# A short first block, a reordered preparation of the scan, GpSimd held back behind two projections, and mLSTM gating one chunk later

## The reference, cut to what matters

```python
z, xbc, dt = jnp.split(h @ w_in, [SSM_D_INNER, SSM_D_INNER + SSM_CONV_DIM], axis=-1)
dt = jax.nn.softplus(dt.astype(f32) + dt_bias.astype(f32))
a = dt * A                        # per head; a_cs = cumsum over a chunk of 128 tokens
decay_to_end = jnp.exp(a_cs[..., -1:] - a_cs)
...
x = x + rmsnorm(y, post_norm[i])  # behind the projections out of mamba and of attention
...
h = num / jnp.maximum(jnp.abs(den), jnp.exp(-m_t))[..., None]        # mLSTM
mh = rmsnorm_2(mh, mlstm_norm_w) * jax.nn.sigmoid(m_o)
```

## Time and profile before

| | |
|---|---|
| median of 3 runs | 2681.82 us (2678.59 to 2682.61) |
| profiled execution, its own time | 2678.74 us |
| span in the profile | 2677.0 us |
| PE, DVE, POOL, ACT busy | 2320.1, 1568.4, 1502.8, 714.9 us |

### The profile page before, as it was taken

One profiled execution on the slowest core, in us unless ns is written; L12 is line 12 of the kernel. 1 busy time (PEld: TensorE's weight loads), 2 busy tenths in 40 slices (PEclk: granted clock), 3 DMA queues, 4 the chain that ended last, 5 costly groups with the idle time before them and its releaser, 6 DMA issues.

```text
span 2677.0 us, 28363 instructions
## 1 busy us (share of the span) xinstructions
PE 2320.1 (87%) x9216; PEld 1519.9 (57%) x9216; DVE 1568.4 (59%) x3381; ACT 714.9 (27%) x1935; POOL 1502.8 (56%) x1060
## 2 busy tenths in 40 slices
PE   8999899899989999789988888888777777777776
PEld 7888678788978879677754443444232223222222
DVE  1266592333431668632387878887778776555555
ACT  2111553214422131423222222222223222111112
POOL 7777377676567754264665656555544444344331
PEclk9999899999989999899999999999999999999999
DMA  4222002222222210031289999999999999999996
GB/s 146 93 95 94 17 1 93 91 100 80 103 88 87 86 63 1 1 110 48 100 339 408 421 421 421 421 413 421 421 422 422 421 421 422 421 422 421 421 421 258
DMA packets 105898, 646.35 MB, mean 241 GB/s; under 512 B 12720, under 2 KB 15152, under 8 KB 39600
## 3 DMA queue, kind: packets, MB, share of 16 engines
q0 software_dynamic: 73728, 536.90, 48.3%
q1 hardware_dynamic: 31776, 106.87, 11.6%
q10 hardware_dynamic: 272, 1.05, 0.1%
HBM read 640.58 MB, written 4.19 MB: 241 GB/s over the span
## 4 chain that ended last, share of the span: by engine, by line
DMA 32%; PE 10%; DVE 5%; POOL 2%; issue 1%; ACT 1%; POOLq 0%; DVEq 0%; ACTq 0%
DMA peer_row<-in_peer_uv,peer_ids 32%; PE bank L3156 7%; DVE peer_row L3101 3%; PE bank L281 2%; POOL peer_row L3078 1%; PE bank L2850 1%; POOL w_parts L229 1%; ACT peer_diag L3135 1%; DVE peer_weight L3093 1%; PE bank L2811 0%; POOL w_parts L227 0%; DVE peer_top_i L2669 0%; DVE peer_picked L2742 0%; DVE peer_sc_left L2672 0%; DVE peer_top_v L2665 0%
## 5 line engine op out<-in xcount | busy, mean ns | idle before, releaser
L3156 PE MATMUL bank<-peer_row,peer_diag 128*128 128x512 f32 x2048 | 966.8, 618 | 266.7 <-ACT peer_diag L3135 264.5
L3078 POOL DMA_INDIRECT peer_row<-in_peer_uv,peer_ids x512 | 585.8, 1144 | 645.6 <-PE bank L3156 604.4
L3156 PEld LDWEIGHTS bank<-peer_row,peer_diag 128*128 128x128 f32 x2048 | 380.0, 194 | 823.5 <-ACT peer_diag L3135 430.0
L3101 DVE CUSTOM_DVE_ANT_0 peer_row<-peer_row,peer_h_tok 128x1024 f32<-128x1024 f32 x512 | 641.0, 1256 | 329.2 <-DMA peer_row<-in_peer_uv,peer_ids 328.3
L208 POOL TENSOR_TENSOR w_parts<-ring,zero 128x1024 fp32r<-128x1024 f32 x156 | 295.5, 1894 | 227.5 <-PE bank L281 112.4
L211 POOL TENSOR_TENSOR w_parts<-ring,w_parts 128x1024 fp32r<-128x1024 f32 x156 | 374.4, 2400 | 29.0 <-POOL w_parts L208 29.0
L3139 ACT ACTIVATE peer_acts<-peer_dots 128x2 f32<-128x2 f32 x256 | 52.1, 204 | 734.0 <-DVE peer_dots L3101 734.0
L3135 ACT ACTIVATE peer_diag<-ident,peer_weight 128x128 f32<-128x128 f32 x512 | 177.5, 394 | 223.8 <-DVE peer_weight L3093 221.1
L257 PE MATMUL bank<-ssm_h_high,w_parts 128*128 128x512 f32 x512 | 157.7, 389 | 0.8 <-DVEq L644 0.8
L257 PEld LDWEIGHTS bank<-ssm_h_high,w_parts 128*128 128x128 f32 x512 | 96.1, 188 | 20.9 <-DVEq L644 1.0
L257 PE MATMUL bank<-hyb_h_high,w_parts 128*128 128x512 f32 x320 | 99.9, 393 | 0.8 <-DVEq L644 0.8
(11 more groups left out here) (559 smaller groups left out, 3803.8 us busy)
## 6 DMA issues: line engine op xcount, KB each, us to landing
ring<-in_weights SPq DMA_DIRECT2D x180, 512.0 KB, 3.2
peer_row<-in_peer_uv,peer_ids POOLq DMA_INDIRECT x512, 25.4
resid<-in_x SPq DMA_DIRECT2D x4, 512.0 KB, 7.6
out<-resid SPq DMA_DIRECT2D x4, 512.0 KB
xa_mem<-in_mem ACTq DMA_DIRECT2D x1, 1024.0 KB, 4.9
xa_kept<-xa_v_out SPq DMA_DIRECT2D x1, 1024.0 KB
xa_kept<-xa_k_out SPq DMA_DIRECT2D x1, 1024.0 KB
xa_v<-xa_kept SPq DMA_DIRECT2D x1, 1024.0 KB, 5.3
```

The lines of the kernel that those rows point to most:

```text
L3078: pool.indirect_dma_start(self.rows[row][:, :], None, self.m.ins["peer_uv"], bass.IndirectOffsetOnAxis(ap=self.choice.ids[:, t, slot:slot ...
L3101: dot = dve.tensor_tensor_reduce(mine, mine, self.tokens(slot_of(j)[0]), 1.0, 0.0, ALU.mult, ALU.add, self.dots[:, h % 4, r:r + 1])
L3156: mm = pe.matmul(self.m.banks[2 * t + half][:, :], self.diag[:, j % (2 * GROUP), :], self.rows[row][:, D + half * 512:D + (half + 1) * 512 ...
```

## The change

It has four parts, and none of them changes what is computed.

1. `set_up` keeps two loads, the first quarter of the tokens and `cols`; nothing waits for `cols` there, ACT does in the next block. All other loads are issued in `mamba_in`, the second quarter now ahead of the first unit. The three small rows for the scan are loaded there too.
2. The preparation of the scan uses seven banks for the transposes; DVE takes the tiles 0 to 3 and the even ones, ACT the odd ones from 5. The bias is added first of all, PE's sums stand behind tile 13, and the exponentials stand between the copies.
3. Behind the two projections GpSimd splits four units by `split_ahead`. Between the high and the low part of the first it waits for the four additions. In the second place the split of the small weight comes after these four units.
4. In mLSTM GpSimd begins to gate chunk t when chunk t + 1 has its denominator.

```diff
-def split_ahead(m, pool, n, parts=None):
+def split_ahead(m, pool, n, parts=None, pause=None):
...
         pool.wait_ge(m.w_high, u + 1)
+        if pause is not None and u == m.split:
+            pool.wait_ge(*pause)
         pool.tensor_tensor(low, m.ring[:, u % RING, :], high, ALU.subtract).then_inc(m.w_split, 1)
...
@@ set_up
-            for n in range(4):
-                here = slice(n * D // 4, (n + 1) * D // 4)
-                sp.dma_start(m.resid[:, :, here], x[:, :, here]).then_inc(m.x_loaded[n], 16)
-                if n == 0:
-                    sp.dma_start(m.cols[:, :], m.ins["cols"]).then_inc(loaded, 16)
-                    sp.dma_start(m.ring[:, 0, :], m.ins["weights"][0]).then_inc(m.w_loaded[0], 16)
-            stream_weights(m, sp, RING)
-            sp.wait_ge(loaded, 16)
+            load_tokens(m, sp, 0)
+            sp.dma_start(m.cols[:, :], m.ins["cols"]).then_inc(m.cols_loaded, 16)
...
@@ mamba_in
+            load_tokens(m, sp, 1)
+            sp.dma_start(m.ring[:, 0, :], ins["weights"][0]).then_inc(m.w_loaded[0], 16)
+            for n in (2, 3):
+                load_tokens(m, sp, n)
+            stream_weights(m, sp, RING)
             sp.dma_start(raw.w[:, :, :], ins["ssm_w_dt"]).then_inc(raw.loaded, 16)
+            for n, name in enumerate(("ssm_dt_bias", "ssm_a_log", "ssm_d")):
+                sp.dma_start(rows[:, n, :], m.row(name, HEADS)).then_inc(rows_loaded, 16)
             stream_weights(m, sp, 4 * ZC + CM_T)
+            sp.wait_ge(rows_loaded, 48)
...
@@ mamba_scan, PE
-                    if j >= 4:
-
-                        pe.wait_ge(by_act if j % 2 else by_dve, (j - 4) // 2 + 1)
+                    before = j - len(turn_banks)
+                    if before >= 0:
+                        pe.wait_ge(by_dve if dve_takes(before) else by_act, taken(before))
...
+                    if j == SUMS_AFTER:
+                        pe.wait_ge(dve_dt, 3)
...
@@ mamba_out_attention_in, gpsimd
             split_weights(m, pool, kt)
-            split_weights(m, pool, project.units)
+            split_ahead(m, pool, RING, pause=(out.added, TT))
+            split_weights(m, pool, project.units - RING)
...
@@ attention_out_hybrid_in, gpsimd
             split_weights(m, pool, kt)
+            split_ahead(m, pool, RING, pause=(out.added, TT))
             split_small(pool, raw.w, raw.parts, raw.loaded, raw.split)
-            split_weights(m, pool, CH * DT // 2 + HC_T)
+            split_weights(m, pool, CH * DT // 2 + HC_T - RING)
...
@@ HeadNorm.gpsimd
-        pool.wait_ge(self.mixed_ready, t + 1)
+        pool.wait_ge(self.mixed_ready, t + 2)
```

78 lines of the change are left out of this document (40 added, 38 removed).

## The result

The changed kernel takes 2661.76 us (median of 4 runs, 2658.84 to 2662.52) where the kernel before took 2681.11 beside it: ratio 0.9927, interval 0.9912 to 0.9943. In a second series it took 2663.91 (5 runs, 2661.46 to 2667.68; ratio 0.9938, 0.9925 to 0.9952). The change is worth 17 us by the means. The profiled execution took 2661.18.

The account below looks back on a forecast made before the run. One core's chain of blocks with PE busy nearly throughout, then gather DMA (32% of the span), was taken as the bound. Terms 0 - 6.9 + 0 - 4.1 - 0.8 = -11.8 us gave 2669, range 2664 to 2675.5.

Parts of the forecast that it names:

- Part 1, the start: Kernel's start, loads issued later: 0 us, bounds -0.5 and +2; the fourth quarter's landing at 12.5 sets the end.
- Part 2, the block: Preparation of the scan: waits among the transposes and the lone chain behind them go, 14.1 us for 21.0, so -6.9.
- The scan's start: PE's clock at the scan's start, after a pause of some 2.8 us for 4.96: 0, bounds -2 and 0.
- Part 3, the stalls: Additions behind two projections: no GpSimd beside them, 1.63 + 0.45 = 2.08 us saved at each place, -4.1 together.
- The rival of the late low part: Behind the additions, PE waits for GpSimd's low part and both places lose all they win: 2673 us, chance 0.06.
- Part 3, the clock: At both additions, PE back after a shorter pause keeps its full clock, about 1 us each; bound -6, chance 0.2.
- Part 4, mLSTM: mLSTM chunks: DVE's additions no longer meet GpSimd's gating, less 0.4 back at the last statistic: -0.8, bounds -1.3 and 0.
- The sum: Whole kernel: 0 - 6.9 + 0 - 4.1 - 0.8 = -11.8 us, giving 2669.
- the local clock case: PE's clock stays up at the scan's start (-2) and each addition (-1): 2665 us, chance 0.2.
- The clock stays up: Rival: PE's shorter pauses in three places keep its clock, -2 at the scan's start, -1 per addition: 2665, chance 0.2.
- Slower: Rival: the gather's steps, some 40 of about 25 us, lengthen; at 1 us more each 2703 us, chance 0.02.

Follow-up runs that it names:

- after_again: The changed kernel run once more, with nothing altered, for its spread and a second trace: median 2663.91 us, ratio 0.9938 to the kernel before.
- first_pause: The kernel before with GpSimd's pause only at the first additions, behind the projection out of mamba: median 2680.56 us, ratio 0.9997.
- before_shift: The kernel before with 16 useless PE transposes in the middle of the projection into the hybrid mixer: median 2681.13 us, ratio 1.0001.
- pauses_shift: The kernel before with GpSimd's pauses at both additions and 11 useless PE transposes in the projection into the hybrid mixer: median 2677.65 us, ratio 0.9987.
- the third place found here: The changed kernel with GpSimd's split in the cross attention's core held until the last weights are scaled: median 2657.95 us, ratio 0.9920 to the kernel before.

## Why the prediction was right in direction and too small

- **Part 1, the start: right in the number** (0 forecast, 0.0 by the mean, good to 0.8), not in the path. The fourth quarter was to set the end at 12.5. PE's last wait ended with the third quarter, at 10.71, and 16 transposes in a row led to 14.04. And the clock, which I had only as a bound, did matter: by their pace the first projection matmuls ran slow (1.20 us for two, 0.71 before). In the seven traces with the new start the projection ends at 101.8 to 103.6 us, in the nine with the old one at 100.8 to 102.6: 1.0 us later on average.
- **Part 2, the block: right.** 14.1 us were forecast with one half-clock spell among the transposes. In after_again, with such a spell, the stage is 1.66 longer than in the first trace, so the block is 12.13 + 1.66 = 13.8. The spell was taken as certain; of the seven traces with the new preparation four had none (13.46 for the stage) and three had one (15.12). A tile at the half clock takes 0.76 us (18 transposes in 3.40), and 0.78 by the row that I read as 0.85. That the part alone measured 7.3 for a forecast of 6.9 is in part luck, as the next step shows.
- **The scan's start: the first step that failed.** I took 0, bounds -2 and 0. PE's pause of 2.34 us never halved the clock there: 22.79 in all seven traces with the new preparation, 24.75 to 25.32 in the nine with the old one. It is worth 2.0 to 2.5 us. Alone, the part still measured 7.3, not 9 to 10. In its trace core and out were 4.7 us longer than in the kernel before, but in first_pause, with the old preparation, they were as long, so that is no explanation; where the other 2 us went stays open.
- **Part 3, the stalls: right in mechanism and place.** Additions of 4.87 (4.86 forecast), L558 at 0.16, the low part ahead of PE, no wait for it. The low part ended 0.90 us ahead of PE's matmul, for 1.4 forecast. The two stages gave 1.5 to 2.9 us each, and only 1.5 of the forecast 2.1 at the same share of half clock. The rival of the late low part is out.
- **Part 3, the clock: the step that failed.** I priced it as a local matter ("back after a shorter pause, keeps its full clock", -1 at each addition) and gave it 0.2. It is not only local. The term was -4.1, bounds -6 to -2; the part measured -7.2, with the first pause at 0 and the second at -6.5. before_shift shows, between two traces alike up to the edit, that 1.8 us more of PE's work decides over 1.6 us at waits some 45 us further on. That it also decides over 3 us at the core's last wait, 480 us behind the second additions, is argued from the raster and from pauses_shift's total, not shown by a clean pair of traces. How the second pause's 6.5 us are made up stays in part open.
- **Part 4, mLSTM: the mechanism right, the size open.** The additions of the later chunks take 0.16, and 0.31 came back in the last L2176 for 0.4 forecast. But 0.8 were forecast, and the measurements go from 3.0 (alone) to about nothing (the changed kernel without it), with 0 to 0.9 in its stage at the same share of half clock.
- **The sum.** By the means 17 us came where 11.8 were forecast. Of the missing 5, 3.1 are the third part's, put down to the clock behind the pauses, and 2.2 the fourth's alone, which is unexplained. The scan's start adds 2 in every trace, and about as much is lost again in the second part's total, at a place not found. The range's low end allowed for the local clock case "less a run's spread", and for nothing behind it.
- **The rivals.** "The clock stays up" came nearest (2665), but it held only at the scan's start: behind the additions the clock fell in both traces of the changed kernel. "Slower" counts its steps as 40 and then, for 2703, as 34; the gather didn't change (1308.3 in both profiles).

## What to carry to other kernels

A DVE instruction that takes several times as long as its like while GpSimd works is worth its excess if PE waits for it: look for such outliers through the whole trace, and hold GpSimd back there by a wait on the later event, as at the third place found here. Price PE's clock over the whole kernel, not at the edit: a saved microsecond moves all later waits, and can return as half-clock stretches elsewhere or take some away; before_shift is the clean case. Compare stages at the same share of half clock, and use several executions, since one trace of this kernel is good to some 3 us in its total.

## What the runs showed of the hardware

- Two traces of the same code differed by 6.5 us, in stages that differ in the granted clock.
- Two waits of 0.78 and 0.84 us, with 1.16 us of PE work between them, were followed by 3.4 us at the half clock when they came at one place of the raster, and not when they came 1.6 us later. In 16 traces the stretch was there at 0.93 to 1.25 us behind a raster point, and not from 1.65 us on.
- Executions that begin anywhere on the raster had come to nearly the same place on it some 740 us in, in 15 of 16 traces. Small changes of PE's work moved a kernel's mean by more or less than their own size: the first pause, worth 1.5 us in its stage, gave 0.2, the second, worth 2.7, gave 6.5. Single executions still differ: the changed kernel's two traces do at the core.
- Useless transposes kept the clock up through both waits behind the projections (0 of 6.8 us at the half clock), and the total was 3.3 us lower in one kernel and 2.7 to 4.0 higher in the other.
- Two DVE scalings of 128x256 took 4.30 us beside GpSimd's split and 0.61 without it.
